# Expert weights in ten equal places in rotation, TensorE's experts written out one by one

## The chip, the cores and the metric

The kernel runs on one core of one Trainium2 chip. The metric is the device time in microseconds (us) of one execution; less is better. Engines: TensorE (PE in the profile; PEld is its weight load), VectorE (DVE), ScalarE (ACT), GpSimd (POOL), and SyncE (SP), whose queue issues nearly all transfers. Sixteen DMA engines carry the transfers.

## The reference

The kernel computes two transformer blocks over 256 tokens of width 1024 in float32. The first ends with a sparse mixture of experts, which the change is about:

```python
def sparse_moe(h, router_w, router_b, w1, b1, w2, b2):
    logits = (hf @ router_w + router_b)
    top_val, top_idx = lax.top_k(logits, TOP_K)        # 4 of 32 experts for each token
    gate = jax.nn.softmax(top_val, axis=-1)
    ...                                                # tokens sorted by expert
    def expert_block(args):
        e, toks, wts = args
        u = hf[toks] @ w1[e] + b1[e]                   # 1024 -> 2 x 1024
        g_, lin = u[:, :D_FF], u[:, D_FF:]
        g_ = jnp.minimum(g_, SWIGLU_LIMIT)
        lin = jnp.clip(lin, -SWIGLU_LIMIT, SWIGLU_LIMIT)
        y = ((lin + 1.0) * g_ * jax.nn.sigmoid(SWIGLU_ALPHA * g_)) @ w2[e] + b2[e]
        return y * wts[:, None]
    ...                                                # and added up by token
```

In front of it stand a normalisation, two attention mixers and an output projection; behind it a second block (attention, MLP, a recurrent layer, a second MLP), whose weights pass through the same ring of places.

## The kernel before

**Passes.** An expert takes at most 64 tokens (`CAP`) in a pass, so an expert with more tokens has two or more passes. Their number is known only after routing: VectorE counts each expert's tokens, and writes the number of passes (`passes`) and each expert's last pass (`lasts`) to SBUF, from where the other engines read them into registers. The plan (`table`) gives each pass its expert and a code for selecting tokens. TensorE turns it from a column into a row (`turn_plan`, L1277) inside the first pass. With these inputs there are 33 passes: expert 5 has two, every other expert one.

**A pass on TensorE** (`expert_pass`, L1344): bias products (L1322), 64 up products against four parts of the first weight (L1340), each part counted off by `w1_parts`; the gather of the next pass's tokens (L1300); the scatter of the last pass's outputs into sums in four PSUM banks (L1313); three sets of transposes (L1379, L1306, L1385); and 32 down products against two parts of the second weight (L1394), counted off by `w2_parts`. The first pass is a form of its own: its bias products are done before it, the plan is turned after its second part, and instead of a scatter it has `base`, 16 products that start the sums with the experts' second bias (L1292). The other passes are a loop on TensorE, VectorE and ScalarE, with a pass number in a register.

**Weights.** An expert has 12 MiB of weights in six parts of 2 MiB, each 128 partitions by 4,096 words. Parts 0 to 3 go to the four places of `ring`, which the stages before and behind use too; parts 4 and 5 go to two places of their own, `w2`. SyncE loads part after part. Before each it waits until that part of the last pass of the expert before has been consumed (`pass_freed`, L145). So the six places always hold parts of one expert or the next.

**Held pieces.** Near 160 us, while the mixers end and before routing is known, SyncE also loads pieces of part 0 of five later experts into memory that the mixers have left: 1,536 of 4,096 words of expert 14, and the whole part of experts 18, 22, 26 and 30 (`HELD`). When such an expert's turn comes, GpSimd copies the piece into the ring in steps of 512 words (L801), and SyncE loads the rest, if there is one (`load_rest`), and goes on from part 1. SyncE's program is a chain of loops between the held experts.

**Hand-over.** After `w1_parts` says that all up products of the last pass are done, SyncE starts to load the second block's weights (`B_LOADS`), four at once.

Of the kernel before, what the change touches and what calls it, by code (L numbers as in the profile page):

```python
# [38 lines left out]
ds = bass.ds  # L39
# [51 lines left out]
HELD = ((14, 1536), (18, 4096), (22, 4096), (26, 4096), (30, 4096))  # L91
PIECE = 512
# [38 lines left out]
B_AT, _ = slot_amounts(B_LOADS, A_N, [n + 16 * EXPERTS for n in A_AMOUNT])  # L131
# [141 lines left out]
class Memory:  # L273


    def __init__(self, nc, ctx):
# [18 lines left out]
        self.table = sb("table", [1, 2, 64], I32)  # L295
        self.lasts = sb("lasts", [1, EXPERTS], I32)
        self.ps = ctx.enter_context(nc.psum_tensor("ps", [P, 8, 512], F32))
# [95 lines left out]
        self.column = a.take(2)  # L393
# [5 lines left out]
        self.seen = a.take(1)  # L399
        bias_at = ARENA - 864 - 2 * D  # L400
        w2_at = bias_at - 2 * SLOT
        held_at = w2_at - sum(words for _, words in HELD)
        assert a.at <= held_at
        a = Area(arena, held_at)
        self.held = [a.take(words) for _, words in HELD]
        self.w2 = a.take(2, SLOT)
# [59 lines left out]

    def block_sum(self, n, half):

        return self.parts[:, n, 0:2 * half].rearrange("p (m n) -> p m n", m=2)
# [28 lines left out]
sel_ready gathered he_ready he_turned hTe_ready selt_done selz_ready selw_ready planned plan_turned w1_parts u_read g_ready sg_ready  # L498
# [11 lines left out]
class Signals:  # L510


    def __init__(self, nc, ctx):
        self.sem = {name: ctx.enter_context(nc.semaphore(name)) for name in SEMAPHORES}
        self.loaded = [ctx.enter_context(nc.semaphore(f"loaded{s}")) for s in range(RING)]
        self.held_loaded = ctx.enter_context(nc.semaphore("held_loaded"))
        self.rest_loaded = ctx.enter_context(nc.semaphore("rest_loaded"))
        self.w2_loaded = [ctx.enter_context(nc.semaphore(f"w2_loaded{s}")) for s in range(2)]
# [5 lines left out]
def program_sync(nc, sp, m, s, a):  # L524
# [91 lines left out]
    def load_held(j):  # L616

        expert, words = HELD[j]
        src = a["exp_w1"][0, expert, 0:2 * P, :].rearrange("(p k) n -> p (k n)", p=P)
        sp.dma_start(m.held[j], src[:, 0:words]).then_inc(s.held_loaded, 16)  # L620

    def load_rest(j):

        expert, words = HELD[j]
        r = A_N % RING
        last = sp.value_load(m.lasts[0:1, expert - 1:expert], min_val=0, max_val=MAX_PASSES - 1)
        wait_for(pass_freed(last, 0))
        src = a["exp_w1"][0, expert, 0:2 * P, :].rearrange("(p k) n -> p (k n)", p=P)
        sp.dma_start(m.ring[:, r, words:SLOT], src[:, words:SLOT]).then_inc(s.rest_loaded, 16)

    def load_part(part, expert):

        if part < 4:
            r = (A_N + part) % RING
            src = a["exp_w1"][0, ds(expert, 1), 2 * P * part:2 * P * (part + 1), :]
            sp.dma_start(m.ring[:, r, :], src.rearrange("e (p k) n -> p (e k n)", p=P)).then_inc(s.loaded[r], 16)
        else:
            src = a["exp_w2"][0, ds(expert, 1), 512 * (part - 4):512 * (part - 3), :]
            sp.dma_start(m.w2[:, part - 4, :],
                         src.rearrange("e (p k) n -> p (e k n)", p=P)).then_inc(s.w2_loaded[part - 4], 16)  # L640

    for part in range(PASS_LOADS):
        if part == 2:
            sp.wait_ge(s["o_copied"], 8)
            for j in range(len(HELD)):
                load_held(j)
        if part < 4:
            wait_for(a_freed(A_N + part - RING))
        elif part == 4:
            sp.wait_ge(s["split_ready"], 1)  # L650
            sp.wait_ge(s["wout_done"], C)
        load_part(part, 0)
    sp.wait_ge(s["routed"], 1)
    passes = sp.value_load(m.passes[0:1, 0:1], min_val=EXPERTS, max_val=MAX_PASSES)

    def load_expert(expert, from_part=0):

        last = sp.value_load(m.lasts[0:1, ds(expert - 1, 1)], min_val=0, max_val=MAX_PASSES - 1)
        for part in range(from_part, PASS_LOADS):
            wait_for(pass_freed(last, part))  # L660
            load_part(part, expert)
# [12 lines left out]
    sp.wait_ge(s["w1_parts"], passes * 4)  # L674
    for n, load_of in enumerate(B_LOADS):
        if n >= RING:
            wait_for(b_freed(n - RING))
        load(B_AT[n][0], load_of, s.loaded[B_AT[n][0]])
        if load_of == ("up", 1, 0):
            sp.dma_start(m.fgain, a["norm_final_2"].unsqueeze(0).to_broadcast([P, D])).then_inc(s["p1_loaded"], 16)  # L680


def program_gpsimd(nc, pool, m, s, a):
# [83 lines left out]
    link(g.memset(m.seen, 0.0))  # L767
# [21 lines left out]
    pool.wait_ge(s["routed"], 1)  # L789
    r = A_N % RING  # L790
    for j, (expert, words) in enumerate(HELD):
        last = pool.value_load(m.lasts[0:1, expert - 1:expert], min_val=0, max_val=MAX_PASSES - 1)
        name, value = pass_freed(last, 0)
        pool.wait_ge(s[name], value)
        seen = m.seen[0:32, :]
        link(g.tensor_tensor(seen, seen, seen, ALU.subtract))  # L796
        pool.wait_ge(s.held_loaded, 16 * len(HELD))
        if words < SLOT:
            pool.wait_ge(s.rest_loaded, 16)
        for at in range(0, words, PIECE):  # L800
            put = g.tensor_copy(m.ring[:, r, at:at + PIECE], m.held[j][:, at:at + PIECE])  # L801
            if at + PIECE < words:
                link(put)
        put.then_inc(s.loaded[r], 16)
# [51 lines left out]
def program_tensor(nc, pe, m, s, a):  # L856
# [420 lines left out]
    def turn_plan():  # L1277

        pe.wait_ge(s["planned"], 1)
        mm(bank(5)[0:1, P:2 * P], m.column[:, 0:1], ident, start=True, stop=True)  # L1280
        mm(bank(5)[0:1, 2 * P:3 * P], m.column[:, 1:2], ident, start=True, stop=True).then_inc(s["plan_turned"], 1)
        pe.wait_ge(s["weights_ready"], 1)
        for t in range(2):
            last = turn(bank(4)[:, P * t:P * t + P], m.wtile[:, t, :], ident)
        last.then_inc(s["w_turned"], 1)

    def base():
# [3 lines left out]
        for c in range(C):  # L1291
            mm(m.token_sum(c), m.b2[:, P * c:P * c + P], m.wT.rearrange("p t n -> p (t n)"), start=(c % 2 == 0),  # L1292
               stop=False, skip_group_check=True)

# [49 lines left out]
    def expert_pass(p, expert, first=False):  # L1344

        pe.wait_ge(s["hTe_ready"], p + 1)
        if not first:
            biases(0)
        for kk in range(4):
            r = (A_N + kk) % RING  # L1350
            pe.wait_ge(s.loaded[r], expert * 16 + (A_AMOUNT[r] + 16))
            w = m.ring[:, r, :].rearrange("p (k n) -> p k n", n=2 * FF)
            if kk == 0:
                for part in range(2):
                    if part == 1 and not first:
                        pe.wait_ge(s["y_ready"], p)
                        biases(1)
                    for k in range(2):
                        last = up_products(w, k, part)
            else:  # L1360
                for k in (2 * kk, 2 * kk + 1):
                    for part in range(2):
                        last = up_products(w, k, part)
            last.then_inc(s["w1_parts"], 1)
            if first and kk == 1:
                turn_plan()

        pe.wait_ge(s["sel_ready"], p + 2)
        if first:
            gather()  # L1370
            base()
        else:
            pe.wait_ge(s["y_ready"], p)
            pe.wait_ge(s["selz_ready"], p)
            gather()
            scatter()
# [11 lines left out]
        for half in range(2):  # L1388
            pe.wait_ge(s["aT_ready"], p * 2 + (half + 1))
            pe.wait_ge(s.w2_loaded[half], expert * 16 + 16)  # L1390
            w = m.w2[:, half, :].rearrange("p (k n) -> p k n", n=D)
# [11 lines left out]
    pe.wait_ge(s["y_ready"], passes)  # L1403
    pe.wait_ge(s["selz_ready"], passes)
# [383 lines left out]
def program_scalar(nc, act, m, s, a):  # L1788
# [120 lines left out]
    expert_pass(0)  # L1909
    act.wait_ge(s["routed"], 2)  # L1910
    passes = act.value_load(m.passes[0:1, 0:1], min_val=EXPERTS, max_val=MAX_PASSES)
    with act.Fori(1, passes) as p:
# [200 lines left out]
def program_vector(nc, dve, m, s, a):  # L2113
# [314 lines left out]
    v.tensor_copy(m.passes[:], upto[0:1, EXPERTS - 1:EXPERTS])  # L2428
    v.tensor_scalar(m.lasts[:], upto[0:1, :], -1.0, None, ALU.add).then_inc(s["routed"], 1)
# [641 lines left out]
```

## Time and profile before

| what | value |
|---|---|
| median of 3 runs | 1780.75 us (1779.87 to 1781.33) |
| span of the profiled execution | 1779.1 us |
| TensorE busy | 1719.1 us, 97% |
| VectorE busy | 714.1 us, 40% |
| ScalarE busy | 264.1 us, 15% |
| GpSimd busy | 133.3 us, 7% |
| moved | 548.13 MB, 308 GB/s over the span |

The table's median is of whole runs; the rows below are all of one profiled execution, whose only own time is its span. Times in them count from the start of the span. The expert stage lies between 198 and 1,117 us.

### The profile page before, as it was taken

The page shows a single profiled execution, that of the slowest core. Times are in us where ns is not written, and L with a number is a line of the kernel's source. Part 1 is how long each engine was busy: PE and PEld are TensorE (multiplying, and loading weights), DVE is VectorE, ACT ScalarE, POOL GpSimd, SP SyncE. Part 2 cuts the span into 40 slices and gives each one's busy share as a digit, 9 for nine tenths or more (in the row PEclk, how much of TensorE's full clock was granted, in tenths as well). Part 3 has the DMA queues.
Part 4 walks back from the last instruction along what each step waited for, and adds up shares of the span by engine and source line. Part 5 has one row for each costly group of instructions (what it writes and reads, how often), then busy time and mean ns, then how long its engine had stood idle before and what let it go on. Part 6 is the DMA issues. An engine that isn't in the chain of part 4 may idle for free.

```text
span 1779.1 us, 25654 instructions
## 1 busy us (share of the span) xinstructions
PE 1719.1 (97%) x10381; PEld 1062.2 (60%) x10382; DVE 714.1 (40%) x1307; ACT 264.1 (15%) x564; POOL 133.3 (7%) x188
## 2 busy tenths in 40 slices
PE   9999999999999998989999999999999999999998
PEld 6557533333333333333333333797999998899987
DVE  2665412212212121221212122665777545768743
ACT  1145201101101010101101011214111001511100
POOL 4016200000000001001010010200100000010000
PEclk9999999999999999999999999999999999999999
DMA  9988999979999999999999999741344543545440
GB/s 317 355 299 304 413 416 429 398 320 428 430 427 429 429 427 429 429 427 429 429 427 428 429 428 424 258 150 48 116 168 147 186 143 121 199 151 182 166 166 24
DMA packets 98612, 548.13 MB, mean 308 GB/s; under 512 B 6034, under 2 KB 16482, under 8 KB 71826
## 3 DMA queue, kind: packets, MB, share of 16 engines
q1 hardware_dynamic: 98402, 546.93, 76.6%
q8 instruction: 49, 0.80, 0.2%
q10 hardware_dynamic: 144, 0.26, 0.0%
q14 instruction: 17, 0.14, 0.0%
HBM read 546.12 MB, written 1.05 MB: 308 GB/s over the span
## 4 chain that ended last, share of the span: by engine, by line
PE 69%; DMA 28%; ACT 1%; DVE 1%; POOL 0%; SPq 0%; issue 0%; DVEq 0%; POOLq 0%; ACTq 0%
DMA ring<-in_exp_w 28%; PE ps L1340 14%; PE ps L1650 11%; PE ps L1679 6%; PE ps L1720 5%; PE ps L1394 5%; PE ps L1495 4%; PE ps L1421 3%; PE ps L994 2%; PE ps L972 2%; PE ps L1749 2%; PE ps L1221 1%; PE ps L1300 1%; PE ps L1313 1%; PE ps L1774 1%; PE ps L1583 1%
## 5 line engine op out<-in xcount | busy, mean ns | idle before, releaser
L1340 PE MATMUL ps<-ring,sq 128*64 128x512 f32 x2112 | 475.9, 595 | 45.3 <-DMA ring<-in_exp_w 44.7
L1340 PEld LDWEIGHTS ps<-ring,sq 128*64 128x64 f32 x2112 | 146.7, 137 | 350.5 <-issue 252.8
L1394 PE MATMUL ps<-arena,hn 128*64 128x512 f32 x1056 | 233.9, 595 | 0.0
L2479 DVE TENSOR_SCALAR hn<-ps 128x512 f32<-128x512 f32 x33 | 22.8, 692 | 345.4 <-PE ps L1340 345.4
L2406 DVE TENSOR_SCALAR sq<-arena,rstd 128x64 f32<-128x64 f32 x68 | 19.5, 330 | 338.2 <-PE ps L1340 337.5
L1394 PEld LDWEIGHTS ps<-arena,hn 128*64 128x64 f32 x1056 | 72.8, 137 | 137.6 <-issue 137.4
L1898 ACT ACTIVATE sq<-hn 128x512 f32<-128x512 f32 x33 | 20.8, 629 | 532.8 <-DVE hn L2479 532.8
L1650 PE MATMUL ps<-arena 128*128 128x136 f32 (+1 forms) x768 | 90.0, 277 | 0.0
L1650 PEld LDWEIGHTS ps<-arena 128*128 128x128 f32 x768 | 88.6, 191 | 0.0
L1794 ACT ACTIVATE arena<-ps 128x512 f32<-128x512 f32 (+4 forms) x69 | 33.7, 500 | 280.2 <-PE ps L1679 78.4
L2529 DVE TENSOR_TENSOR arena<-ring 128x1024 f32<-128x1024 f32 x37 | 45.7, 1235 | 65.2 <-PE ps L1679 33.5
L1313 PEld LDWEIGHTS ps<-sq 64*128 64x128 f32 x528 | 48.7, 186 | 32.7 <-issue 26.0
L1313 PE MATMUL ps<-sq 64*128 64x256 f32 x528 | 66.9, 390 | 0.8 <-ACT sq L1794 0.7
L812 POOL TENSOR_TENSOR sq<-sq 128x272 f32<-128x272 f32 (+1 forms) x28 | 28.6, 1021 | 498.0 <-ACT sq L1920 295.5
L1300 PE MATMUL ps<-arena,sq 128*64 128x512 f32 x272 | 64.2, 592 | 0.2 <-DVE arena L2408 0.2
L1794 ACT ACTIVATE sq<-ps 64x256 f32<-64x256 f32 x66 | 32.2, 488 | 207.0 <-PE ps L1394 206.6
L1679 PE MATMUL ps<-arena 128*128 128x136 f32 x512 | 61.9, 279 | 0.0
L796 POOL TENSOR_TENSOR arena<-arena 32x1 f32<-32x1 f32 x5 | 0.9, 183 | 804.9 <-PE ps L1340 804.9
L1650 PE MATMUL ps<-hn,ring 128*128 128x136 f32 (+1 forms) x512 | 60.8, 277 | 0.0
L1679 PEld LDWEIGHTS ps<-arena 128*128 128x128 f32 x512 | 60.5, 190 | 0.0
L1650 PEld LDWEIGHTS ps<-hn,ring 128*128 128x128 f32 x512 | 59.6, 191 | 0.1
L1720 PE MATMUL ps<-arena 128*128 128x256 f32 x256 | 57.9, 379 | 0.0
(442 smaller groups left out, 2282.8 us busy)
## 6 DMA issues: line engine op xcount, KB each, us to landing
ring<-in_exp_w SPq DMA_DIRECT2D x123, 2048.0 KB, 22.8
arena<-in_exp_w SPq DMA_DIRECT2D x68, 2048.0 KB, 21.4
ring<-in_mlp_w_up SPq DMA_DIRECT2D x16, 2048.0 KB, 7.5
ring<-in_mlp_w_down SPq DMA_DIRECT2D x16, 2048.0 KB, 7.8
ring<-in_ada_w SPq DMA_DIRECT2D x8, 2048.0 KB, 8.7
ring<-in_sb_w_qkv SPq DMA_DIRECT2D x6, 2048.0 KB, 14.0
ring<-in_ada_w SPq DMA_DIRECT2D x8, 1024.0 KB, 10.8
ring<-in_lru_w_in SPq DMA_DIRECT2D x4, 2048.0 KB, 8.3
```

The costliest lines, as they stand in the source:

```text
L972: last = mm(bank(z_bank(v))[:, 0:w], m.hn[:, k, META + P * t:META + P * t + P], wt[:, kk, c0:c0 + w], start=(k == 0), stop=(k == C - 1))
L1300: last = mm(bank(0)[64 * h:64 * h + 64, :], m.sel[:, t, :], m.h2[:, t, 512 * h:512 * h + 512], start=(t == 0), stop=(t == 1))
L1313: return mm(m.token_sum(c), m.y[rows, P * (c % 4):P * (c % 4) + P], m.selz[rows, h, :], start=False, stop=stop, skip_group_check=True)
L1340: last = mm(bank(2 + part)[64 * h:64 * h + 64, :], lhs, w[:, k % 2, at:at + 512], start=False, stop=(k == C - 1))
L1394: last = mm(bank(3)[64 * h:64 * h + 64, :], m.aT[:, q, 64 * half:64 * half + 64], w[:, q, 512 * h:512 * h + 512], start=(half == 0 and q = ...
L1421: last = mm(bank(banks[q] if banks else b0 + q)[:, lo:TT], w[:, k, P * q:P * q + P], act[:, k, lo:TT], start=(n == 0), stop=(n == C - 1))
L1495: last = mm(bank(qkv_bank(n, j))[:, half * f:half * f + half], weights_of(weights, w, m.wsum[:, n % 2], k)[:, P * f:P * f + P], inputs_of( ...
L1650: last = mm(bank(set_bank(n, j))[:, half * f:half * f + half], weights_of(weights, w, m.wsum[:, n % 2], k)[:, P * f:P * f + P], inputs_of( ...
L1679: last = mm(bank(b)[:, half * f:half * f + half], weights_of(weights, w, m.wsum[:, n % 2], k)[:, P * f:P * f + P], hidden_of(tokens, 0, gr ...
L1720: last = mm(bank(b)[:, 0:256], hidden_of(tokens, 1, group, k), weights_of(weights, w, m.wsum[:, n % 2], k), start=(group == 0 and k == 0), ...
L1794: f(dst, src, ACT.Copy, scale=scale).then_inc(s[name], 1)
L2529: link(v.tensor_tensor(t1, w[:, 0, :, 1], w[:, 0, :, 0], ALU.subtract))
```

## The change

- There are ten equal places (`EXPERT_SLOTS`): the four of the ring and six in the memory of the held pieces and `w2`. The 192 parts of all experts, in order, go to places 0 to 9 in rotation; part n waits for part n - 10. `HELD`, `load_held`, `load_rest` and GpSimd's copies are gone.
- Early loads: parts 0 and 1, then at the point of the held pieces parts 6 to 9, then 2, 3, and 4, 5.
- SyncE's loads are written out without loops. The first two of the second block go to places that expert 30's parts 2 and 3 leave; the next two to those of expert 31's parts 4 and 5.
- TensorE's program has a body for each of the 32 experts, and around it a loop over that expert's passes, whose bounds come from a new row `upto`.
- The first pass has the general form: its bias products and a scatter are inside it. For this GpSimd sets `y` and the scatter matrix `selz` to zero ahead of it, and four products of zeros open the sums (`open_sums`). The plan is turned, and `base` is done, between the passes of expert 0 and those of expert 1.
- VectorE makes a short table for expert 0's passes first (from `numbers`), runs those passes, then works out the plan of all passes (one column, no longer two), then runs the others. ScalarE's loop begins at pass 0.

```diff
-HELD = ((14, 1536), (18, 4096), (22, 4096), (26, 4096), (30, 4096))
+EXPERT_SLOTS = 10
+EXPERT_LOADS = EXPERTS * PASS_LOADS
...
+def expert_amount(n):
+    slot, turn = n % EXPERT_SLOTS, n // EXPERT_SLOTS
+    return 16 * (turn + 1) + (A_AMOUNT[ring_of(slot)] if slot < RING else 0)
...
+B_FIRST = A_N + 2
+B_AT, _ = slot_amounts(B_LOADS, B_FIRST, E_AMOUNT)
...
+        far_at = w2_at - (EXPERT_SLOTS - RING - 2) * SLOT
+        self.far = Area(arena, far_at).take(EXPERT_SLOTS - RING, SLOT)
...
+    def expert_slot(self, n):
+        slot = n % EXPERT_SLOTS
+        if slot < RING:
+            return self.ring[:, ring_of(slot), :]
+        return self.far[:, (slot - RING - 2) % (EXPERT_SLOTS - RING), :]
...
 SyncE:
-    begin = 1
-    for j, (held, words) in enumerate(HELD):
-        with sp.Fori(begin, held) as expert:
-            load_expert(expert)
-        if words < SLOT:
-            load_rest(j)
-        load_expert(held, from_part=1)
-        begin = held + 1
-    with sp.Fori(begin, EXPERTS) as expert:
-        load_expert(expert)
-    sp.wait_ge(s["w1_parts"], passes * 4)
+    for n in (0, 1):
+        wait_for(a_freed(A_N + n - RING))
+        load_part(n)
+    sp.wait_ge(s["o_copied"], 8)
+    for n in range(6, 10):
+        load_part(n)
+    for n in (2, 3):
+        wait_for(a_freed(A_N + n - RING))
+        load_part(n)
+    sp.wait_ge(s["split_ready"], 1)
+    sp.wait_ge(s["wout_done"], C)
+    for n in (4, 5):
+        load_part(n)
+    sp.wait_ge(s["routed"], 1)
+    for n in range(EXPERT_SLOTS, EXPERT_LOADS):
+        expert, part = divmod(n - EXPERT_SLOTS, PASS_LOADS)
+        if part == 0 or n == EXPERT_SLOTS:
+            last = last_pass(expert)
+        wait_for(pass_freed(last, part))
+        load_part(n)
+    before_last, last = last_pass(EXPERTS - 2), last_pass(EXPERTS - 1)
+    freed_by = [(before_last, 2), (before_last, 3), (last, 4), (last, 5)]
     for n, load_of in enumerate(B_LOADS):
-        if n >= RING:
-            wait_for(b_freed(n - RING))
+        wait_for(b_freed(n - RING) if n >= RING else pass_freed(*freed_by[n]))
...
 GpSimd:
-    for j, (expert, words) in enumerate(HELD):
...
-        for at in range(0, words, PIECE):
-            put = g.tensor_copy(m.ring[:, r, at:at + PIECE], m.held[j][:, at:at + PIECE])
...
+    pool.wait_ge(s["norm_summed"], 2)
+    g.memset(m.y, 0.0).then_inc(s["y_ready"], 1)
+    pool.wait_ge(s["y_ready"], 1)
+    g.memset(m.selz, 0.0).then_inc(s["selz_ready"], 1)
...
 TensorE:
+    def open_sums():
+        pe.wait_ge(s["y_ready"], 1)
+        zero = m.y.bitcast(BF16)
+        for b in range(4, 8):
+            mm(bank(b), zero[:, 0:P], zero[:, 0:512], start=True, stop=False, skip_group_check=True)
...
     gather()
+    open_sums()
     pe.wait_ge(s["split_ready"], 1)
-    biases(1)
     pe.wait_ge(s["he_ready"], 1)
     turn_gathered()
-    pe.wait_ge(s["routed"], 1)
-    biases(0)
...
-    expert_pass(0, 0, first=True)
-    passes = pe.value_load(m.passes[0:1, 0:1], min_val=EXPERTS, max_val=MAX_PASSES)
-    with pe.Fori(1, passes) as p:
-        expert_pass(p, pe.value_load(m.table[0:1, 1, ds(p, 1)], min_val=0, max_val=EXPERTS - 1))
+    pe.wait_ge(s["routed"], 1)
+    begin = 0
+    for expert in range(EXPERTS):
+        end = pe.value_load(m.upto[0:1, expert:expert + 1], min_val=expert + 1, max_val=MAX_PASSES)
+        with pe.Fori(begin, end) as p:
+            expert_pass(p, expert)
+        if expert == 0:
+            turn_plan()
+            base()
+        begin = end
...
 VectorE:
+    v.tensor_copy(m.upto[:], upto[0:1, :])
...
+    v.tensor_scalar(more, numbers, needed[0:1, 0:1], float(EXPERTS), ALU.is_lt, ALU.mult)
+    link(v.tensor_scalar(other, numbers, needed[0:1, 0:1], None, ALU.is_equal))
+    link(v.tensor_tensor(more, more, numbers, ALU.mult))
+    link(v.tensor_tensor(m.table[0:1, 0:CHUNKS + 1], more, other, ALU.add))
...
+    own = dve.value_load(m.upto[0:1, 0:1], min_val=1, max_val=CHUNKS)
+    with dve.Fori(0, own) as p:
+        expert_pass(p)
...
+    v.tensor_reduce(m.column, code, AX.X, ALU.add).then_inc(s["weights_ready"], 1)
+    dve.wait_ge(s["w_turned"], 1)
+    link(v.tensor_copy(m.table[:], bank(2)[0:1, 0:64]))
+    v.tensor_copy(m.wT, bank(2)[:, P:3 * P].rearrange("p (t n) -> p t n", t=2)).then_inc(s["w_placed"], 1)
     passes = dve.value_load(m.passes[0:1, 0:1], min_val=EXPERTS, max_val=MAX_PASSES)
-    with dve.Fori(1, passes) as p:
+    with dve.Fori(own, passes) as p:
         expert_pass(p)
```

## Rows read from the trace of the kernel before

**Rows 1.** The page: TensorE's busy time, and the DMA share in 40 slices.

```profile
PE 1719.1 (97%) x10381; PEld 1062.2 (60%) x10382; DVE 714.1 (40%) x1307; ACT 264.1 (15%) x564; POOL 133.3 (7%) x188
...
DMA  9988999979999999999999999741344543545440
```

**Rows 2.** The page: the chain that ended last, by engine.

```profile
PE 69%; DMA 28%; ACT 1%; DVE 1%; POOL 0%; SPq 0%; issue 0%; DVEq 0%; POOLq 0%; ACTq 0%
```

**Rows 3.** Windows: stretch, length; busy us (instructions) by engine; clock, DMA share, GB/s.

```profile
252.00:278.00 26.00, 26.00 (x136) 10.15 (x134) 5.41 (x11) 2.64 (x6) 0.00 (x0) 1.00 1.00 427
...
345.00:356.00 11.00, 10.15 (x58) 4.81 (x60) 4.25 (x6) 2.04 (x5) 0.00 (x0) 1.00 0.70 299
356.00:366.00 10.00, 10.00 (x52) 3.43 (x50) 0.55 (x3) 0.60 (x1) 0.00 (x0) 1.00 0.00 0
...
371.00:740.00 369.00, 349.37 (x1770) 131.66 (x1768) 72.38 (x145) 34.59 (x79) 7.11 (x13) 1.00 1.01 428
```

**Rows 4.** The chain of waits, 196 to 372 us: start, length, what.

```profile
198.21 7.09 PE ps L1340 x32
205.30 0.31 PE ps L1280 x2
...
206.20 7.02 PE ps L1340 x32
...
214.93 3.65 PE ps L1292 x16
...
226.69 0.22 PE ps L1322 x2
...
252.76 0.22 PE ps L1322 x2
...
278.83 0.22 PE ps L1322 x2
...
361.40 0.22 PE ps L1322 x2
```

**Rows 5.** SyncE's timeline, 120 to 480 us: start, stretch, loads issued.

```profile
160.01 2.69 SPq L620 DMA_DIRECT2D arena<-in_exp_w  x5
...
202.05 11.67 SPq L636 DMA_DIRECT2D ring<-in_exp_w  x4
...
328.77 3.76 SPq L639 DMA_DIRECT2D arena<-in_exp_w  x2
365.45 10.63 SPq L636 DMA_DIRECT2D ring<-in_exp_w  x4
```

**Rows 6.** Queue 8, first 223 to 226 us, then 1,134 to 1,779: packets, MB, share.

```profile
q8 instruction: 1, 0.02, 2.1%
...
q8 instruction: 36, 0.59, 0.4%
```

**Rows 7.** The only queue of instructions in 250 to 1,110 us.

```profile
q14 instruction: 1, 0.01, 0.0%
```

**Rows 8.** The chain of waits, whole span: up products of some experts' last parts.

```profile
534.71 3.68 PE ps L1340 x16
...
564.08 3.68 PE ps L1340 x16
...
709.19 3.65 PE ps L1340 x16
...
763.79 3.68 PE ps L1340 x16
```

**Rows 9.** VectorE in the timeline, 183 to 272 us: the copies of table and weights.

```profile
205.93 0.28 DVE L2459 CAST table<-ps 1x128 int32<-1x128 f32 x1 [4.05 <-PE ps L1281]
...
206.23 0.42 DVE L2462 COPY root<-ps 128x256 f32<-128x256 f32 x1
```

**Rows 10.** The timeline, 1,085 to 1,145 us: second block's first loads and products.

```profile
1105.34 32.25 SPq L568 DMA_DIRECT2D ring<-in_sb_w_qkv  x5
...
1120.98 11.27 PE L1421 MATMUL ps<-hn,ring 128*128 128x272 f32 x48
```

More of the change, by code:

```diff
@@ L294, in __init__ @@
         self.passes = sb("passes", [1, 1], I32)
-        self.table = sb("table", [1, 2, 64], I32)
+        self.table = sb("table", [1, 64], I32)
         self.lasts = sb("lasts", [1, EXPERTS], I32)
+        self.upto = sb("upto", [1, EXPERTS], I32)
         self.ps = ctx.enter_context(nc.psum_tensor("ps", [P, 8, 512], F32))
@@ L392, in __init__ @@
         self.plan = a.take(6, EXPERTS)
-        self.column = a.take(2)
+        self.column = a.take(1)
         self.rowno = a.take(1)
@@ L398, in __init__ @@
         self.index = a.take(EXPERTS)
-        self.seen = a.take(1)
+        self.early = a.take(2, CHUNKS + 1)
+        self.numbers = a.take(CHUNKS + 1)
         bias_at = ARENA - 864 - 2 * D
         w2_at = bias_at - 2 * SLOT
[L402 to L406, printed above, removed]
+        far_at = w2_at - (EXPERT_SLOTS - RING - 2) * SLOT
+        assert a.at <= far_at
+        self.far = Area(arena, far_at).take(EXPERT_SLOTS - RING, SLOT)
         assert early_all <= bias_at - 2 * FF
@@ L515, in __init__, with expert_loaded @@
         self.loaded = [ctx.enter_context(nc.semaphore(f"loaded{s}")) for s in range(RING)]
-        self.held_loaded = ctx.enter_context(nc.semaphore("held_loaded"))
-        self.rest_loaded = ctx.enter_context(nc.semaphore("rest_loaded"))
-        self.w2_loaded = [ctx.enter_context(nc.semaphore(f"w2_loaded{s}")) for s in range(2)]
+        self.far_loaded = [ctx.enter_context(nc.semaphore(f"far_loaded{s}")) for s in range(EXPERT_SLOTS - RING)]
+    def expert_loaded(self, n):
+        slot = n % EXPERT_SLOTS
+        return self.loaded[ring_of(slot)] if slot < RING else self.far_loaded[slot - RING]
     def __getitem__(self, name):
@@ L631, in load_part @@
[L631 removed]
+    def load_part(n):
+        expert, part = divmod(n, PASS_LOADS)
         if part < 4:
[L634 to L640 removed]
@@ L642, in program_sync @@
[L642 to L652, printed above, removed]
-    sp.wait_ge(s["routed"], 1)
-    passes = sp.value_load(m.passes[0:1, 0:1], min_val=EXPERTS, max_val=MAX_PASSES)
@@ L766, in program_gpsimd @@
     link(g.memset(m.wt, 0.0))
-    link(g.memset(m.seen, 0.0))
+    link(g.iota(m.numbers, pattern=[[1, CHUNKS + 1]], base=0, channel_multiplier=0,
+                allow_small_or_imprecise_dtypes=True))
     g.memset(m.wtile, 0.0).then_inc(s["pool_moe"], 1)
@@ L1342, in up_products, with expert_pass, part @@
         return last
-    def expert_pass(p, expert, first=False):
+    def expert_pass(p, expert):
+        def part(k, words):
+            n = PASS_LOADS * expert + k
+            pe.wait_ge(s.expert_loaded(n), expert_amount(n))
+            return m.expert_slot(n).rearrange("p (k n) -> p k n", n=words)
         pe.wait_ge(s["hTe_ready"], p + 1)
-        if not first:
-            biases(0)
+        biases(0)
         for kk in range(4):
-            r = (A_N + kk) % RING
-            pe.wait_ge(s.loaded[r], expert * 16 + (A_AMOUNT[r] + 16))
-            w = m.ring[:, r, :].rearrange("p (k n) -> p k n", n=2 * FF)
+            w = part(kk, 2 * FF)
             if kk == 0:
-                for part in range(2):
-                    if part == 1 and not first:
-                        pe.wait_ge(s["y_ready"], p)
+                for half in range(2):
+                    if half == 1:
+                        pe.wait_ge(s["y_ready"], p + 1)
                         biases(1)
                     for k in range(2):
-                        last = up_products(w, k, part)
+                        last = up_products(w, k, half)
             else:
                 for k in (2 * kk, 2 * kk + 1):
-                    for part in range(2):
-                        last = up_products(w, k, part)
+                    for half in range(2):
+                        last = up_products(w, k, half)
             last.then_inc(s["w1_parts"], 1)
-            if first and kk == 1:
-                turn_plan()
         pe.wait_ge(s["sel_ready"], p + 2)
[L1369 to L1376, printed above, removed]
+        pe.wait_ge(s["selz_ready"], p + 1)
+        gather()
+        scatter()
         pe.wait_ge(s["a_ready"], p + 1)
@@ L1389, in expert_pass @@
             pe.wait_ge(s["aT_ready"], p * 2 + (half + 1))
-            pe.wait_ge(s.w2_loaded[half], expert * 16 + 16)
-            w = m.w2[:, half, :].rearrange("p (k n) -> p k n", n=D)
+            w = part(4 + half, D)
             for q in range(4):
@@ L1907, in expert_pass @@
         copy(m.y, bank(3), "y_ready")
-    expert_pass(0)
-    act.wait_ge(s["routed"], 2)
+    act.wait_ge(s["routed"], 1)
     passes = act.value_load(m.passes[0:1, 0:1], min_val=EXPERTS, max_val=MAX_PASSES)
-    with act.Fori(1, passes) as p:
+    with act.Fori(0, passes) as p:
         expert_pass(p)
@@ L2432, in program_vector @@
     turned_gather()
-    link(v.tensor_tensor(first, upto, needed, ALU.subtract))
-    link(v.tensor_scalar(behind, first, -1.0, m.rowno, ALU.mult, ALU.add))
-    link(v.tensor_tensor(inside, needed, behind, ALU.is_gt))
-    link(v.scalar_tensor_tensor(inside, behind, 0.0, inside, ALU.is_ge, ALU.mult))
-    link(v.scalar_tensor_tensor(code, behind, float(EXPERTS), m.index, ALU.mult, ALU.add))
-    link(v.tensor_tensor(code, code, inside, ALU.mult))
-    link(v.tensor_reduce(m.column[:, 0:1], code, AX.X, ALU.add))
-    link(v.tensor_tensor(code, m.index, inside, ALU.mult))
-    v.tensor_reduce(m.column[:, 1:2], code, AX.X, ALU.add).then_inc(s["planned"], 1)
+    more, other = m.early[0:1, 0, :], m.early[0:1, 1, :]
+    numbers = m.numbers[0:1, :]
+    v.tensor_scalar(more, numbers, needed[0:1, 0:1], float(EXPERTS), ALU.is_lt, ALU.mult)
+    link(v.tensor_scalar(other, numbers, needed[0:1, 0:1], None, ALU.is_equal))
+    link(v.tensor_tensor(more, more, numbers, ALU.mult))
+    link(v.tensor_tensor(m.table[0:1, 0:CHUNKS + 1], more, other, ALU.add))
     for c in range(1, CHUNKS):
```

77 lines of the change are left out of this document (27 added, 50 removed).

## The prediction, made before the changed kernel was run

> **What bounds the kernel now.** I read the page first, then the windows of the expert stage, then the chain of waits, then SyncE's own timeline. The page says that TensorE is busy for 97% of the span and the transfers for most of it until shortly after 1,100 us [rows 1], and the chain that ended last gives 28% of the span to transfers [rows 2]. Both engines look full, so the question is which of them sets the pace, and where. The windows answer it: from 371 us on the 16 DMA engines are at share 1.01 and 428 GB/s without a hole, while TensorE has some idle time in them (349 busy of 369) [rows 3]. One expert's weights are six parts of 2 MiB. In the steady stretch one expert's last up part is consumed 29.37 us after that of the expert before (534.71 to 564.08) [rows 8], so a part costs the DMA 29.37 / 6 = 4.895 us. A pass that waits for nothing takes 26.07 us (252.76 to 278.83) [rows 4]. TensorE is therefore 3.3 us per expert faster than the weights, and the stage is bound by transfers, except just after a place where TensorE used more time than one pass for an expert.
>
> There is exactly one such place. SyncE refills places after each expert's last pass; its groups follow each other by some 26 to 29 us, but after the two loads at 328.77 the next comes only at 365.45 [rows 5]. So expert 5 has two passes, 5 and 6, and frees nothing in the first. In that time everything in SBUF fills up and the DMA stops: 299 GB/s in 345 to 356, then exactly 0 in 356 to 366 [rows 3]. After it the DMA never rests. So the end of the expert stage is the moment at which the DMA resumes (one issue after the first part of pass 6), plus the bytes still to come times a fixed rate, plus a fixed tail. These three terms are what the change has to move.
>
> **The change part by part.**
>
> *Places.* Before, 6 rotating places plus pieces of 1,536 and four times 4,096 words held for experts 14, 18, 22, 26 and 30: 10.375 places' worth. After: 10 places. This pool is smaller by 0.375, not larger; only its order differs. When the DMA has filled all it may, before has loaded experts 0 to 5 (36 parts) and 4.375 held ones, 40.375; after has parts 0 to 39, that is 40. Left to load: 151.625 parts before, 152 after. Does the DMA after really fill all ten before it may go on? It has 30 parts to bring from about 205.5 (the group of early loads is done a few us after the issue at 202.05 [rows 5]), 30 x 4.895 = 147 us, plus some 2 us lost while pass 0 holds its places: 354 us. The first part of pass 6 is consumed only at 364. So yes, with 10 us (2 parts) to spare, and the hole stays. Term: 0.375 x 4.895 = **+1.8 us**.
>
> *Resume time.* Before, pass 1 begins at 226.69 and pass 6 at 361.40 [rows 4]. Five unhindered passes are 130.35, which would give 357.04: TensorE waited 4.36 us for weights in passes 4 and 5. After, ten places in line give it more ahead there, and I expect these waits to go. Against this, the first pass gets longer. It begins at 198.21 with its bias products instead of having them done before, and has the general pass's length: 224.28. Then comes what stood inside it before: turning the plan and the weights (205.30 to 206.20, 0.90 [rows 4]); VectorE's copy of the table and of the weights, 0.28 and 0.42 [rows 9], now linked and waited for by TensorE, 0.9 with the handoffs where it was hidden under products before; and the 16 bias sums, 3.65 (214.93) [rows 4]. The scatter of a zeroed y takes the place that these sums had in the pass and is in the 26.07. Pass 1 then begins near 229.9 to 230.3 (+3.4), pass 6 near 360.5. The DMA resumes 0.9 us earlier: **-0.9 us**, with ends of -1.3 (all handoffs hidden) and +1.5 (value loads and loop entries cost TensorE some 0.4 us at each of six boundaries; before, a value load stood at each pass too and the 26.07 holds it).
>
> Four zero products that open the sums (0.22 each, as the bias products at 226.69 [rows 4]) fall into TensorE's wait for VectorE between gather and turning; their price if not covered is 0.9 us less the 0.4 of the bias products that leave the place. VectorE's chain for the plan moves behind pass 0's last copy and lies under seven us of down products; without that cover it costs 1.6.
>
> *Code.* TensorE's loop body is written out 32 times. A pass is 136 products and 134 weight loads [rows 3]. In the second block 36 instruction packets of 16 KB were fetched for TensorE [rows 6], and none in 250 to 1,110 us, where queue 8 does not appear beside the one packet of queue 14 [rows 7]. So the loop runs from what the engine already holds. Some 9,300 products and loads for 36 packets are about 260 instructions a packet; the changed kernel fetches about 1.1 packets per expert, 28 in the saturated stretch of experts 6 to 31. One takes 2.1% of 16 engines in 3 us [rows 6], 1.0 us of one DMA engine, in which that engine brings no weights. A part is complete only when its slowest engine is. What such a packet costs is seen once before: between the last up parts at 709.19 and 763.79 lie 54.60 us [rows 8]; two experts less one held part are 58.74 - 4.90 = 53.84. The one packet of queue 14 (8 KB) in the stretch is what else happened: 0.76 us that never came back. So 28 fetches cost between 28 x 1.0 / 16 = 1.8 (spread evenly) and 28 us (all on one engine). I take nearly even, at most two or so per engine, since nothing ties a queue's packets to one engine and queue 1 uses them all: **+2.1 us**. SyncE's loop is written out too, over 150 loads; about five 8 KB packets where one was: **+0.5 us**, between 0 and 3.
>
> In their own sentences: the Trainium skill ("Runtime: NRT & Kernel Launch", Instruction fetch mechanics) says that code streams in 16 KB blocks and that crossing a block is mostly hidden, and that a taken branch out of a small window stalls. By it the fetches cost nothing and the sum would be 2.6 us smaller; the rows agree on the 16 KB but show the 0.76 us of a fetch in a saturated stretch.
>
> *GpSimd.* The held pieces' copies and their semaphores go. GpSimd is busy 7% of the span and nobody on the chain waits for it; nothing is gained, nothing is late. Its two memsets move ahead of pass 0, before the sums that need them.
>
> *Hand-over to the second block.* The first two of its loads may now start when expert 30's parts are free. Before, all were issued at 1105.34 while the last parts were still landing, and TensorE took up the first product at 1120.98 behind ScalarE's scaling, not behind a load [rows 10]. The queue is in order and full either way: 0.
>
> Sum: +1.8 - 0.9 + 2.1 + 0.5 = **+3.5 us**. The profiled span is 1779.1 against a median of 1780.75 for the runs, 1.6 outside the span; 1779.1 + 3.5 + 1.6 = 1784.2.
>
> **The rivals.**
> 1. *Fetches are free.* Each is absorbed by slack of its engine. For: engines need not be equally loaded. Against: 0.76 us in rows 8. Then +1.8 - 0.9 = +0.9, 1781.7. This is also the page's rule above. 0.22.
> 2. *Fetches bunch.* On four engines, seven each: +7 in place of 2.1, 1789; on one, 1810. No row excludes it. 0.15.
> 3. *Boundaries stall TensorE.* Reading `upto` and entering a loop with newly fetched code costs 1 us per expert. In the saturated part the 3.3 us of slack swallow it, but six boundaries before pass 6 delay the resume: +6, 1790. For: fresh code at each. Against: TensorE's sequencer covers the table's value load in each pass now. 0.10.
> 4. *The hole shrinks* (faster). If fewer than 40 parts have landed when pass 6 frees its first, the DMA keeps working through expert 5's double pass, which is what four more rotating places would do where the lead is used up. From 2 parts fewer on it decides; a hole of 10 us closed is -10 + 2.6 + 1.8, about 1775. Against: the lead in passes 0 to 5 is counted above, and whatever fills early is the same pool. 0.08.
>
> **How the numbers follow.** Forecast 0.45, its own range 1782.8 to 1786. What a measurement can tell from no change is 0.2%, 3.6 us, so the bound to slower is 1784.3, in the midst of the forecast. Slower: nearly half of the forecast, rivals 2 and 3: 0.47. Same: the rest of the forecast and rival 1: 0.45. Faster: rival 4, 0.08. The range leaves out rival 4 and the far ends of 2 and 3: 1780.8 to 1791.
>
> **What would show it.** In the profile after: pass 6 begins at 360 to 361, with no waits for weights in passes 1 to 5; the DMA is at 0 GB/s for some 10 to 12 us before 365; from there on 428 GB/s to the end of the stage and 4.9 us per part; queue 8 has some 33 more packets; the end of the last expert's products lies 3 to 4 us later, and all behind it keeps its length. I am wrong if the hole is gone, if passes 1 to 5 take longer than 26.1 us, or if the cadence of 29.37 grows by much more than 0.1 us per expert.

## The result and the profile after

The changed kernel takes 1786.55 us (median of 5 runs, 1786.36 to 1787.71) against 1780.75 for the kernel before (5 runs): ratio 1.0036, 95% interval 1.0025 to 1.0047, some 5.8 us slower. The prediction said 1784.2, range 1780.8 to 1791. The profiled execution's span is 1785.5 us against 1779.1, 6.4 more; the sums below are made against these two. The profiled execution of the changed kernel took 1787.32 us, 0.8 above the median, so its 6.4 is somewhat more than the 5.8 of the medians.

The page of the kernel after, which answers to [rows 1, 2]:

```profile
PE 1721.9 (96%) x10398; PEld 1064.8 (60%) x10399; DVE 710.6 (40%) x1310; ACT 264.2 (15%) x564; POOL 112.7 (6%) x150
...
DMA  9989999989999999999999999641244543545440
...
PE 76%; DMA 22%; ACT 1%; DVE 1%; POOL 1%; issue 0%; POOLq 0%; DVEq 0%; ACTq 0%
```

TensorE is busy for 2.8 us more, about what the four zero products and the first pass's scatter (1.93 us) add; whether that is on the path has to be read from the stages. Nor may the smaller share of DMA in the chain mislead: with ten places a load can be issued more than one and a half experts before it is used, which may be why the chain goes through TensorE more often (not shown). Who sets the pace is read from the windows (columns as in [rows 3]):

```profile
345.00:356.00 11.00, 11.00 (x64) 5.03 (x62) 4.25 (x6) 2.04 (x5) 0.00 (x0) 1.00 0.76 322
356.00:366.00 10.00, 10.00 (x50) 3.38 (x48) 1.15 (x5) 0.60 (x1) 0.00 (x0) 1.00 0.13 26
...
371.00:740.00 369.00, 358.07 (x1834) 137.83 (x1832) 74.47 (x149) 36.93 (x84) 0.00 (x0) 1.00 1.01 428
740.00:1105.00 365.00, 328.90 (x1646) 120.89 (x1644) 65.94 (x137) 31.65 (x72) 0.00 (x0) 1.00 1.01 428
```

The hole in expert 5's double pass is still there, a little shorter, mostly since the DMA resumes earlier, and after it the DMA is as full as before. From SyncE's timeline and the chain of waits of the kernel after:

```profile
311.93 22.53 SPq L653 DMA_DIRECT2D arena<-in_exp_w  x6
364.07 10.63 SPq L653 DMA_DIRECT2D ring<-in_exp_w  x4
```

```profile
225.98 3.72 PE ps L1286 x16
230.04 1.72 PE ps L1339 x8
...
360.38 1.72 PE ps L1339 x8
...
1107.77 3.65 PE ps L1339 x16
```

Pass 1's up products begin at 230.04 where it was 226.91, the first product behind the bias products at 226.69 [rows 4]. Five passes of 26.07 later (130.34 in all) pass 6 begins without any wait, at 360.38, where it was 361.62. SyncE's first refill behind the hole goes out at 364.07 instead of 365.45 [rows 5]. So at this point the changed kernel is 1.4 us ahead. At the last expert's last up part it is behind: 1107.77 against 1101.65 (the same view of the kernel before), 6.1 us. The second block's first product is at 1127.10 against 1120.98 [rows 10], again 6.1, and the rest adds 0.3. All of the loss, and 1.4 more, arises between 364 and 1,108 us, in the stretch in which the DMA never rests. Its queues there, 370 to 1,105 us:

```profile
q1 hardware_dynamic: 21556, 313.85, 100.4%
q8 instruction: 28, 0.46, 0.3%
q14 instruction: 3, 0.02, 0.0%
```

There are 28 packets of TensorE's code, where [rows 7] have none, and three of 8 KB where they have one.

How these hurt can be seen in the records of the loads' semaphores. Each load counts its semaphore up by 16, once for each DMA engine, and as long as no code is fetched the 16 counts keep nearly the same distances from load to load. Here are the 16 counts of single loads in microseconds after the load's first, sorted. The loads are the second one behind the hole and the last of expert 31's up parts, kernel before and kernel after, and between them the loads around two fetches of the changed kernel.

```
before, after the hole  0.00 0.24 0.37 0.38 0.43 0.45 0.46 0.49 0.50 0.53 0.55 0.56 0.71 0.74 0.82 0.84
before, expert 31       last three: 0.73 0.83 1.53
after, after the hole   0.00 0.16 0.17 0.19 0.21 0.22 0.24 0.31 0.34 0.35 0.37 0.40 0.42 0.45 0.50 1.30
after, one fetch later  0.00 0.15 0.18 0.19 0.20 0.23 0.25 0.31 0.35 0.36 0.37 0.39 0.42 0.50 1.31 2.14
after, load at 625.72   0.00 0.01 0.04 0.13 0.18 0.21 0.27 0.74 1.41 1.66 1.77 1.78 1.87 2.67 3.09 3.41
after, load at 630.62   0.00 0.01 0.04 0.12 0.18 0.21 0.28 0.73 1.65 1.76 1.79 1.87 2.68 2.97 3.09 3.42
after, expert 31        0.00 0.15 0.22 0.23 0.24 0.31 0.44 2.25 4.82 4.96 4.96 5.05 6.09 6.28 6.66 7.43
```

Between 625.72 and 630.62, where one packet of 16 KB is fetched (at 627.9), 14 of the 15 counts behind the first stay within 0.01 us, 1.41 is gone and 2.97 is new: one engine has been set back by 1.56 us. (The first pair alone, around the packet at 390.7, would also fit two engines set back by 0.8 each; two loads on, the counts end in 0.51, 1.29 and 2.00, which again is one engine moved by 1.56, from 0.44.) Read in this way from load to load, each of the 28 packets sets one engine back by some 1.5 us, though the packet itself is recorded with 1.0 to 1.1 us, and each of SyncE's three packets of 8 KB sets one back by 0.72.

At the end seven engines have been held up by no code. One has taken SyncE's three packets (2.25). Eight have taken TensorE's 28 in turn, four engines three each (4.82 to 5.05) and four engines four each (6.09 to 7.43). A load is complete with its slowest engine. That engine was the last one already at the hole (1.30), and four packets of 1.53 brought it to 7.43. In the kernel before, the one 8 KB packet fell on the slowest engine, from 0.87 to 1.58, and nothing else happened.

### The profile page after: what moved, and what is told of

The parts are those of the page before. It is cut to its first block, busy times and chain, and to the rows that moved or that the text cites. A ratio compares the mean times of both kernels' runs of the same rounds, so it can differ in the third digit from the quotient of the medians.

```text
span 1785.5 us, 25135 instructions
## 1 busy us (share of the span) xinstructions
PE 1721.9 (96%) x10398; PEld 1064.8 (60%) x10399; DVE 710.6 (40%) x1310; ACT 264.2 (15%) x564; POOL 112.7 (6%) x150
## 4 chain that ended last, share of the span: by engine, by line
PE 76%; DMA 22%; ACT 1%; DVE 1%; POOL 1%; issue 0%; POOLq 0%; DVEq 0%; ACTq 0%
DMA arena<-in_exp_w 15%; PE ps L1339 13%; PE ps L1650 11%; PE ps L1388 9%; DMA ring<-in_exp_w 7%; PE ps L1679 6%; PE ps L1720 5%; PE ps L1495 4%; PE ps L1421 3%; PE ps L1314 3%; PE ps L1301 2%; PE ps L990 2%; PE ps L968 2%; PE ps L1749 2%; PE ps L1217 1%; PE ps L1374 1%
## 5 line engine op out<-in xcount | busy, mean ns | idle before, releaser
L1339 PE MATMUL ps<-arena,sq 128*64 128x512 f32 x1216 | 274.5, 595 | 30.2 <-DMA arena<-in_exp_w 29.9
L1339 PE MATMUL ps<-ring,sq 128*64 128x512 f32 x896 | 201.9, 595 | 18.1 <-DMA ring<-in_exp_w 17.8
L1339 PEld LDWEIGHTS ps<-arena,sq 128*64 128x64 f32 x1216 | 84.4, 137 | 205.9 <-issue 145.3
L1339 PEld LDWEIGHTS ps<-ring,sq 128*64 128x64 f32 x896 | 62.4, 137 | 146.8 <-issue 108.5
L1388 PE MATMUL ps<-arena,hn 128*64 128x512 f32 x640 | 141.7, 595 | 0.0
L1388 PEld LDWEIGHTS ps<-arena,hn 128*64 128x64 f32 x640 | 44.1, 137 | 83.4 <-issue 80.0
L1388 PE MATMUL ps<-ring,hn 128*64 128x512 f32 x416 | 92.1, 595 | 0.0
L1650 PEld LDWEIGHTS ps<-arena 128*128 128x128 f32 x768 | 88.6, 191 | 0.0
L1301 PE MATMUL ps<-arena,sq 128*64 128x512 f32 x272 | 64.2, 593 | 0.2 <-DVE arena L2407 0.2
L1388 PEld LDWEIGHTS ps<-ring,hn 128*64 128x64 f32 x416 | 28.7, 137 | 54.2 <-issue 52.0
```

Of the source, the lines that this page charges most:

```text
L1301: last = mm(bank(0)[64 * h:64 * h + 64, :], m.sel[:, t, :], m.h2[:, t, 512 * h:512 * h + 512], start=(t == 0), stop=(t == 1))
L1339: last = mm(bank(2 + part)[64 * h:64 * h + 64, :], lhs, w[:, k % 2, at:at + 512], start=False, stop=(k == C - 1))
L1388: last = mm(bank(3)[64 * h:64 * h + 64, :], m.aT[:, q, 64 * half:64 * half + 64], w[:, q, 512 * h:512 * h + 512], start=(half == 0 and q = ...
L1650: last = mm(bank(set_bank(n, j))[:, half * f:half * f + half], weights_of(weights, w, m.wsum[:, n % 2], k)[:, P * f:P * f + P], inputs_of( ...
```

## The experiments

Two theories. **A**: the end of the expert stage is the moment at which the DMA resumes behind the double pass, plus the parts still to load at 4.9 us, plus what code fetches take from the slowest DMA engine; the last is the loss. **B**: the rotation of ten places, the first pass's form or the loads' deep queue makes the transfers slower in themselves, and the code is innocent. The kernel before had a median of 1780.75 us beside the changed kernel, 1780.51 beside experiments 1, 2, 4 and 5, and 1780.86 beside 3, 6 and 7; differences from the changed kernel are therefore good to some 0.4 us.

**1. The written-out code alone undone.**

```diff
-    for expert in range(EXPERTS):
-        end = pe.value_load(m.upto[0:1, expert:expert + 1], ...)
-        with pe.Fori(begin, end) as p:
-            expert_pass(p, expert)
...
+    passes_of(0, begin=0)
+    turn_plan()
+    base()
+    passes_of(1)
+    with pe.Fori(0, 6) as group:
+        for j in range(2, 7):
+            passes_of(j, group * 48, at=group * 5 + j)
```

> The changed kernel with TensorE's 32 bodies folded into experts 0 and 1 and a loop of six turns over five bodies (ten places and six parts come round after five experts). Everything else stays written out. Theory A (the fetches of TensorE's code take time from the DMA engines): in 370 to 1,105 us queue 8 falls from 28 packets to none, the last expert's last up part comes some 5 to 6 us earlier than the changed kernel's 1107.8, and the time is 1780.5 to 1781.5. Theory B (the place count, the first pass's form or the deep rotation itself slows the transfers): no fetches, but the time stays at 1786.

Measured 1782.39 us; ratio to the kernel before 1.0011 (1.0002 to 1.0020), 4.2 us below the changed kernel; span 1780.5, 5.0 below. Queues of this kernel in 370 to 1,105 us, and from its chain expert 31's last up part:

```profile
q8 instruction: 2, 0.03, 0.0%
q14 instruction: 3, 0.02, 0.0%
```

```profile
1102.75 3.65 PE ps L1339 x16
```

It comes 5.0 us earlier than 1107.77, with SyncE's resume at 364.18, as in the changed kernel (364.07). The places, the first pass and the deep queue are all still in this kernel, and so is a value load and a loop entry for each expert (here two value loads), so their number isn't the cost either. The time is a little above the 1780.5 to 1781.5 expected, and two packets of queue 8 are left where none was expected: the fetches taken out were worth 4.2 us by the medians and 5.0 by the spans, rather than the 5 to 6 that I took from the counts. What is left of the backlog here is 2.38 us on one engine, which has taken all three packets of SyncE's code (0.72 each).

**2. The written-out code alone done**, on the kernel before.

```diff
-    with pe.Fori(1, passes) as p:
-        expert_pass(p, pe.value_load(m.table[0:1, 1, ds(p, 1)], ...))
...
+    for expert in range(1, EXPERTS):
+        end = pe.value_load(m.table[0:1, 1, expert:expert + 1], ...)
+        with pe.Fori(begin, end) as p:
+            expert_pass(p, expert)
+        begin = end
```

> The kernel before, with its own places, held pieces and first pass, in which only TensorE's loop is written out, one body for each of experts 1 to 31. For these inputs, in which expert 0 has a single pass. Theory A: some 28 fetches in the saturated stretch cost the slowest DMA engine 5 to 6 us, so 1785.5 to 1787. Theory B: 1780.8, as before.

Measured 1786.17 us, ratio 1.0029 (1.0018 to 1.0041): 5.7 us above the kernel before, with its six places and its held pieces. Its queues, again 370 to 1,105 us, and its chain around one late part:

```profile
q8 instruction: 28, 0.46, 0.3%
q14 instruction: 1, 0.01, 0.0%
```

```profile
766.19 3.68 PE ps L1340 x16
...
795.57 3.68 PE ps L1340 x16
...
826.48 3.65 PE ps L1340 x16
...
1107.06 3.65 PE ps L1340 x16
```

From expert to expert it is 29.38 us as in [rows 8] (766.19 to 795.57), but 30.91 in the next, 1.54 more. In it the slowest engine's count goes from 3.55 (load at 806.66) to 5.10 (load at 811.56), with one packet of 16 KB at 811.6; the second slowest stays at 3.54. So a single packet delays the whole stage by its full 1.5 us when it falls on the slowest engine. Such steps add up to an end at 1107.06, 5.4 us after the 1101.65 of the kernel before, while its resume (365.69) is 0.2 later. Theory B can't explain this: none of its parts is in this kernel.

**3. Half written out.** Experts 0 to 16 have bodies of their own, the others are a loop of three turns over five bodies.

> The changed kernel with experts 0 to 16 written out and the others in a loop of three turns over five bodies. Theory A: the cost grows with the number of fetches, so about 15 to 17 packets of queue 8 in 370 to 1,105 us in place of 28 and 2, and 1784 to 1785, between the two. Rival (what costs is a loop entry or a branch, not the fetch): the same number between, but without the delay of single parts where a packet is fetched.

Measured 1784.89 us, ratio 1.0025 (1.0016 to 1.0034). There are 18 packets:

```profile
q8 instruction: 18, 0.29, 0.2%
```

Of these, 16 lie in 370 to 760 us and two behind. With 2, 18 and 28 packets expert 31's last up part is at 1102.75, 1105.32 and 1107.77, and the times are 1782.39, 1784.89 and 1786.55: 0.16 to 0.25 us for each packet. That is what packets of 1.5 us cost if they fall on eight engines in turn (1.55 / 8 = 0.19). The rival, a cost of entering a loop, isn't excluded by this number, but it is by experiment 1, which has as many entries as the changed kernel, and by the landings. Here is the load of expert 31's last up part in four kernels, whose places and resume are the same (us; "spread" is from its first engine to its slowest):

| kernel | packets of queue 8 | first engine | spread | up part consumed from |
|---|---|---|---|---|
| changed | 28 | 1100.29 | 7.43 | 1107.77 |
| half written out | 18 | 1100.23 | 5.04 | 1105.32 |
| five bodies | 2 | 1100.33 | 2.38 | 1102.75 |
| both loops (experiment 6) | 2 | 1100.44 | 2.36 | 1102.84 |

The first engine comes at the same time in all four. All of the difference is in the spread.

**4. Eight places in place of ten.**

```diff
-EXPERT_SLOTS = 10
-B_FIRST = A_N + 2
-    for n in range(6, 10):
-    freed_by = [(before_last, 2), (before_last, 3), (last, 4), (last, 5)]
+EXPERT_SLOTS = 8
+B_FIRST = A_N + 0
+    for n in range(6, EXPERT_SLOTS):
+    freed_by = [(before_last, 4), (before_last, 5), (last, 0), (last, 1)]
```

> The changed kernel with eight places in place of ten. Theory A (the pool counts only by what it holds when the DMA stops in expert 5's double pass): two parts more are left after it, 2 x 4.9 = 9.8 us, so 1796.3, with the resume at the same time. Theory B (any pool that is deep enough for a pass does): 1786.5. Theory C (a shallower pool also makes TensorE wait before the double pass): more than 1797.

Measured 1796.30 us, ratio 1.0089 (1.0075 to 1.0103): 9.75 us above the changed kernel, 4.9 for each place, with pass 6 beginning at the same time (360.41; in the changed kernel 360.38). This is the price forecast for the pool: what counts is how much it holds when the DMA stops. (Between the two profiled executions the step is 9.0, span 1794.5. The first engine of expert 31's last up part comes 9.73 later, 1110.02, and the spread is 0.8 smaller, 6.63.)

**5. The bias sums moved out of the way.**

```diff
         if expert == 0:
             turn_plan()
-            base()
+            pe.wait_ge(s["w_placed"], 1)
+        if expert == 12:
+            base()
```

> The changed kernel with the 16 bias sums (3.65 us) moved from behind expert 0 to behind expert 12, where TensorE waits for weights anyway; the wait for VectorE's copies stays behind expert 0. Theory A (the end of the stage is the moment at which the DMA resumes, plus what is left at a fixed rate): expert 5's second pass begins 3.7 us earlier and the time falls by 3.5 to 3.7, to 1783. Theory B (the stage is bound by all bytes from its beginning, so TensorE's early work is hidden): no change, 1786.5.

Measured 1783.74 us, ratio 1.0020 (1.0011 to 1.0029), 2.8 us below the changed kernel. Theory A holds, its size was 0.9 too high. Pass 6's up products begin at 357.64, only 2.7 us earlier. (The spans differ by 3.7, 1781.8 against 1785.5, which looks like the forecast but isn't: 2.8 are the earlier resume and 0.96 a smaller spread, 6.47 against 7.43.) The chain shows why:

```profile
225.57 0.44 DVE root L2498
226.00 0.88 issue
226.89 0.41 PE ps L1323 x2
```

Between VectorE's copy and TensorE's next product the program has only value loads and a loop entry, and with the sums gone these 0.88 us lie bare. The 3.65 us of sums fall behind expert 12 into waiting for weights and cost nothing there.

**6. SyncE's loop as well**, on the kernel of experiment 1: `for n in range(EXPERT_SLOTS, EXPERT_LOADS)` becomes `with sp.Fori(0, 6) as group` over 30 parts, with addresses from a register.

> The kernel with five bodies, in which SyncE's refills are a loop of six turns over 30 parts too. Theory A: the 8 KB packets of queue 14 in 370 to 1,105 us fall from three to none or one; each cost one DMA engine some 0.75 us, but only the slowest engine counts, so 0 to 1.5 us less than the kernel with five bodies, 1781 to 1782.4. Rival: addresses from registers make SyncE's issues late; then more than 1783.

Measured 1782.16 us, ratio 1.0009 (1.0000 to 1.0018). The three packets of queue 14 are gone, and 0.2 us with them, which is no difference that can be told: expert 31's last up part is at 1102.84, where it was 1102.75. The landings show why: with five bodies the slowest engine was the one that took the three small packets (2.38). Here it is another, which took one of TensorE's two packets of 16 KB and ends at 2.36.

**7. Both loops, and a shorter way to the double pass.**

```diff
-        mm(bank(2)[0:1, 0:P], m.column, ident, start=True, stop=True)
+        mm(bank(1)[0:1, 0:P], m.column, ident, start=True, stop=True)
...                                  (the turned weights and VectorE's reads likewise)
     passes_of(0, begin=0)
     turn_plan()
-    base()
-    passes_of(1)
     with pe.Fori(0, 6) as group:
-        for j in range(2, 7):
+        for j in range(1, 6):
             passes_of(j, group * 48, at=group * 5 + j)
+    base()
+    passes_of(31)
```

> Both loops as in the kernel before this one, and three changes ahead of expert 5's second pass: the 16 bias sums go behind expert 30; the plan and the weights are turned into PSUM bank 1, which the next pass doesn't write at once, so that TensorE no longer waits for VectorE's copies (0.7 us) and its value load isn't laid bare (0.9 us). Theory A (resume plus remainder): pass 6 begins near 355.5 to 356.5, 4 to 5 us earlier than the changed kernel's 360.4; time 1776.5 to 1777.5, below the kernel before. Rival: the sums before the last expert cost their 3.65 us there, since its weights are all that the stage still waits for; then 1780.

Measured 1777.40 us, ratio to the kernel before 0.9983 (0.9974 to 0.9992): the fastest of all, 9.2 us below the changed kernel. From the chain, the first line of pass 6, and TensorE's timeline around the last two experts:

```profile
355.58 0.22 PE ps L1338 x2
```

```profile
1075.78 7.09 PE L1403 MATMUL ps<-arena,hn 128*64 128x512 f32 x32
1082.80 3.72 PE L1301 MATMUL ps<-root,arena 128*128 128x256 f32 x16
...
1097.75 3.65 PE L1354 MATMUL ps<-arena,sq 128*64 128x512 f32 x16 [0.38 <-DMA arena<-in_exp_w]
```

Pass 6 begins 4.6 us earlier than the 360.17 of the changed kernel, SyncE resumes at 359.64, and the time falls 4.8 below the kernel with both loops. The landings agree: the first engine of expert 31's last up part comes 4.4 us earlier (1096.01 against 1100.44), and the spread is 1.69 instead of 2.36. The sums ahead of the last expert just fit: TensorE still waits 0.38 us for the last part.

## Why the prediction was right, and which term was mis-sized

The measured 1786.55 us lies within the stated range, and the change has the direction forecast. It is 0.55 above the forecast's own range (1782.8 to 1786), and the change of +5.8 is well over the +3.5 of the sum.

*The bound: right.* In all eight kernels run the end of the stage is the resume, what is left at a fixed rate, and on top of these the backlog that code leaves on the slowest engine. For the two profiles: the first engine of the second load behind the hole lands 1.1 us earlier than before (375.99 against 377.12). Its way to expert 31's last up part is 1.35 longer. The spread there is 5.9 larger (7.43 against 1.53). That makes the 6.1 us.

*Places, +1.8.* Not measured alone; experiment 4 gives the price of one place as 4.9 us, as taken, and so 1.8 for 0.375. The 1.35 above is the nearest row.

*Resume, -0.9: right.* -1.2 by pass 6's first up product, -1.4 by SyncE's issue. Pass 1 was 3.1 later against the 3.4 forecast, and the 4.36 us of waits in passes 4 and 5 went. The kernel with both loops has these two terms and few fetches: 1782.16 against 1780.86, +1.3, where +0.9 was the forecast for them. Of this some 0.8 is again code, one 16 KB packet on its slowest engine (spread 2.36 against 1.53).

*SyncE's code, +0.5: wrong, and small.* Three packets came, not five. All three fell on one engine, 0.72 us each, which was never the slowest, so in the changed kernel they cost nothing. The kernel before had its one packet on its slowest engine, where it cost 0.7.

*TensorE's code, +2.1: the mis-sized term.* The number of packets was right to the packet (28). Both factors of its price were too low. A packet was taken at 1.0 us, its own duration, and set its engine back by 1.5. "I take nearly even, at most two or so per engine" was wrong too: half of the engines took all of them, and the slowest took four. Four times 1.53 is 6.1 us on the slowest engine. Alone, the written-out code measured 5.7 us added to the kernel before and 4.2 taken from the changed one. Rival 2 was given 0.15 and had the right direction, fewer engines than 16; its numbers (four engines, seven packets of 1.0 each, 1789) were not met. With 5 to 6 in place of 2.1 the sum is 6.4 to 7.4 above 1779.1, and the span says 6.4.

*A sign that was met.* The prediction called itself wrong if the cadence of 29.37 grew by much more than 0.1 us per expert. By the slowest engine's landings, from the second load behind the hole to expert 31's last up part, it grew by 0.2 (from 29.41 to 29.61), and the last products ended 6.1 later instead of 3 to 4. The sign pointed at the right term. The other signs came as said: pass 6 at 360.2, no waits in passes 1 to 5, 33 more packets (82 against 49), though the DMA was silent for some 9 us, not 10 to 12.

*The 1.6 us outside the span.* Runs listed with both their time and their span have 2.1 before and 1.8 after. This moves the forecast by a few tenths.

*Rival 1, free fetches: fallen.* The Trainium skill ("Runtime: NRT & Kernel Launch", Instruction fetch mechanics) calls the cost of crossing a 16 KiB block mostly hidden. For TensorE's own issue the trace agrees: passes 1 to 5 take 130.34 us together (230.04 to 360.38), five times 26.07, while five packets of its code are fetched between 226 and 364 us. For the DMA engines, where they are the bound, experiments 1 and 2 measure 4 to 6 us, for 26 blocks taken out and 28 put in.

*Rival 3, stalls at boundaries: fallen*, by the same 130.34, except where nothing covers the value load and loop entry (0.88 us, experiment 5).

*Rival 4, the hole shrinks: fallen.* All 40 parts had landed before pass 6; the last of them at 355.0, and the 26 GB/s in 356 to 366 are what follows the resume at 364. The ten places held nearly as much as the six and the pieces before.

*GpSimd and the hand-over, 0: right.* The first loads of the second block may start 29 us earlier (1076.41), and its first product comes as long after the last expert's as before.

Open: which engines a queue's code packets go to and why half of them are spared; and why a packet recorded with 1.0 to 1.1 us sets its engine back by 1.5. No kernel here could steer that.

## What to carry to other kernels

In a stretch where transfers are the bound, written-out code is a transfer too, and here it was not shared evenly: the slowest DMA engine counts, so fold code to what the engine can hold and see the instruction queue fall to nothing (here five bodies left two packets, both before 410 us). A pool of buffers that fills completely at one place is worth what it holds at that moment (4.9 us for each place here); after that only an earlier resume, fewer bytes or a better rate help. Work that stands ahead of such a place is on the path even if the engine that does it is not the bound, and the same work behind it was free here (experiment 5), as far as the engine has slack there.

## What the runs showed of the hardware that was not expected

A 16 KB code packet takes 1.0 us of one DMA engine in the records [rows 6], 1.0 to 1.1 in the changed kernel, but sets that engine back by some 1.5 us in a stretch where all engines are full; an 8 KB packet is recorded with 0.31 us and sets it back by 0.72. Counted so, 28 packets took some 43 us of engine time from eight engines, three or four packets each, and the slowest lost 6.1. All packets of the other code queue in that stretch fell on one engine, a ninth.

The backlog stays. In the kernel before the spread was 0.84 to 0.87 us from the hole to 752 us and 1.5 from the packet at 754.6 to the end. Engines do not level out while loads are queued. What took most of it away was the hole, in which all engines ran empty: the spread went from 2.7 us before it to 0.84 behind it in the kernel before, and from 1.9 to 1.3 in the changed one.
